# A hybrid attention/state-space trunk on one core: the scan's own-chunk product made with exchanged operands in three of four head groups

## The chip, the cores and the metric

The kernel runs on one core of one Trainium2 chip. The metric is the device time of one execution, in microseconds. All data is float32; large products are split into three float32r products (high by high, low by high, high by low part).

## The reference, cut to what matters

The program is two mixer layers (an attention layer, then a Mamba-2 scan layer), each with a gated feed-forward behind it, for one sequence of 512 tokens and a model width of 1024. The change touches only the scan of the second mixer:

```python
def step(state, inp):                       # one chunk of 128 tokens
    xc, dtc, bc, cc = inp
    cum = jnp.cumsum(dtc * A, axis=1)
    seg = cum[:, :, None] - cum[:, None]
    L = jnp.exp(jnp.where(tril, seg, -jnp.inf))
    xdt = xc.astype(f32) * dtc[..., None]
    cb = jnp.einsum('btgn,bsgn->btsg', cc, bc)
    y_diag = jnp.einsum('btsgh,bsghp->btghp', cb[..., None] * L, xdt)
    y_off = jnp.einsum('btgn,bghpn->btghp', cc, state) * jnp.exp(cum)[..., None]
    decay = jnp.exp(cum[:, -1:] - cum)
    new_state = (state * jnp.exp(cum[:, -1])[..., None, None]
                 + jnp.einsum('bsgn,bsghp->bghpn', bc, xdt * decay[..., None]))
    return new_state, y_diag + y_off
```

There are 32 heads of width 64 in four groups of eight, four chunks of 128 tokens, and a state of 128 per head. `y_diag` is the chunk's own y. After the scan, y gets a skip term, is multiplied by silu(z), normalised over its group, and projected.

## The kernel before

The instructions of each engine are written out by hand and ordered with semaphores; there is no scheduler. The scan part is unrolled: the outer loop runs over the head groups g = 0 to 3, the inner over the chunks k = 0 to 3. `last` means g = 3.

For each (g, k) the tensor engine (PE) does, in this order: `chunk_products(g, k + 1)` (two small products that give C·B and the turned B of the next chunk, lines 995 and 996); filler of place 0; a wait for `y_done` of the chunk before; the state's share of y (line 1062, bank 3) and the state's update (line 1065, bank 4); **the chunk's own y** (line 1071, bank 2): eight products, one for each head, with the 128x128 decay matrix `Lx` stationary and the 64 columns of scaled x, `xdt`, moving; filler of place 1; `to_features(g, k - 1)`, four transposes of the finished y of the chunk before (line 1003); filler of place 2. A float32 product of this kind is two instructions in the trace, so eight products are 16 there.

Filler is, in groups 0 to 2, the projection of z for the next group (line 1019): 24 products with 512 columns for each chunk, in thirds of eight. The table `places` puts the thirds at (none; two; one) for k = 0, (one; one; one) for k = 1 and 2, and (two; one; none) for k = 3. In group 3 the filler is the first half of the output projection (lines 476 to 478).

The vector engine (DVE) collects y in `ybuf`: state's share times decay (line 2067, not for k = 0), state update (2069, 2070, or 2072 for k = 0), plus the own y from bank 2 (2076), plus the skip term (2078, not for k = 0), times `zs` = silu(z) (2081), which signals `y_done`. The scalar engine (ACT) runs, for each (g, k): at k = 0 `split_hi` (1116, high part of a weight chunk); `z_copy` (1453); `decays(g, k + 1)` (1417, eight times, and 1423), which gives the decay matrices of the next chunk; `stage(g, k + 2)` (1408); at k = 0 of groups 1 to 3 the silu of z for the whole group (1482, with a table load); at k = 3 another `split_hi`; and then, waiting for `y_done`, the square of y (1503). GpSimd (POOL) scales x and multiplies `Lx` with C·B (2251 to 2259).

PSUM has eight banks. In the scan, banks 0 and 5 take z, 2 to 4 the parts of y, 6 and 7 the small products and the transposes. Bank 1 holds a tile of the first z projection, read by the four silu of line 1513 before the scan begins, and is next used in group 3.

Of the kernel before, what the change touches and what calls it, by code (L numbers as in the profile page):

```python
# [23 lines left out]
F32 = mybir.dt.float32  # L24
# [4 lines left out]
ACT = mybir.ActivationFunctionType  # L29
AX = mybir.AxisListType.X  # L30

P = 128
# [9 lines left out]
SH, SG, SHP, SP_, SN = 32, 4, 8, 64, 128  # L42
# [106 lines left out]
def trunk(nc, wstream, xT_in, cols_in, rows_in, pos_in, cw1_in, cw2_in, ident_in, tri_in, cmask_in, out):  # L149
    with ExitStack() as ctx:  # L150
# [3 lines left out]
        def sem(name):  # L154
            return ctx.enter_context(nc.semaphore(name))


        class Region:
# [29 lines left out]
        a = Region(scratch_at)  # L188
# [70 lines left out]
        zs = a.take("zs", [P, TT, GW])  # L259
        dt_at = a.end + 2 * TT * SH * 4  # L260
        dtb = a.take("dtb", [P, 10, TT * SH])
        dt_f = a.take("dt_f", [SH, SEQ])
        ex_at = a.end
        ex = a.take("ex", [P, 3, TT * SH])
# [62 lines left out]
        cum_copied, cumT_mm, cumT_done, rows_stored = map(  # L327
            sem, ("cum_copied", "cum_transposed", "cumT_copied", "cum_rows_stored"))
        row_landed = [sem("even_row_landed"), sem("odd_row_landed")]
        half_free, cs_read = sem("first_weights_free"), sem("cmp_scores_read")  # L330
        gate_in, gate_done, hh_done, hl_done = map(sem, ("gate_normed", "gate_done", "hidden_hi_done", "hidden_lo_done"))
        vec, pool_self = map(sem, ("vector_step", "pool_step"))
# [138 lines left out]
        def _(pe):  # L471
# [534 lines left out]
            def group(g, last):  # L1006
                def z_part(tt, third):

                    if third == 0:
                        if tt == 0:  # L1010
                            pe.wait_ge(lo_done, g * 2 + (n0 + 3))
                        pe.wait_ge(evac, g * 4 + (t0 + 4 + tt - 1))
                    t = slice(tt * P, (tt + 1) * P)
                    for m in range(8 * third, 8 * third + 8):
                        kt, pss = divmod(m, 3)
                        slot, w = (n0 + kt // 4) % 2, slice((kt % 4) * 512, (kt % 4 + 1) * 512)
                        if m == 12 and tt == 0:
                            pe.wait_ge(lo_done, g * 2 + (n0 + 4))
                        ins = mm(ps[:, z_bank_of(tt), :], (xh, xl, xh)[pss][:, kt, t], (wh, wh, wl)[pss][:, slot, w],  # L1019
                                 start=m == 0, stop=m == 23)  # L1020
                        if tt == 3 and m in (11, 23):
                            ins.then_inc(products, 2)
                        elif m == 23:
                            ins.then_inc(z_mm, 1)


                def half_product(t, ks):

                    c, m = divmod(t, 2)
                    n = CHUNK["ssm_out"] + c  # L1030
                    bank = half_bank(t)
                    if ks[0] == 0:
                        if t < 2:
                            pe.wait_ge(evac, EVAC["ssm_out"] - 1 + (t == 0))
                        pe.wait_ge(lo_done, n + 1)
                        after(pe, half_stored, t - 2)
                    for kt in ks:
                        if t == 0 and kt % 2 == 0:
                            pe.wait_ge(yl_done, kt // 2 + 1)
                        w = slice(kt * 256 + m * P, kt * 256 + (m + 1) * P)  # L1040
                        hi, lo = ys(kt)
                        ins = split_product(ps[:, bank, :].rearrange("p (a b) -> p a b", b=P), (wh[:, n % 2, w], wl[:, n % 2, w]),
                                            (hi, lo), kt == 0, kt == FIRST_KT - 1)
                    if ks[-1] == FIRST_KT - 1:
                        ins.then_inc(products, 1)

                places = {0: ((), (0, 1), (2,)), 1: ((0,), (1,), (2,)), 2: ((0,), (1,), (2,)), 3: ((0, 1), (2,), ())}
                for k in range(TT):
                    if k < 3 or not last:
                        chunk_products(g, k + 1)  # L1050

                    def z_at(place):
                        for third in () if last else places[k][place]:
                            z_part(k, third)
                        for t in FILL_AT.get((k, place), ()) if last else ():
                            half_product(*t)
                    z_at(0)
                    after(pe, y_done, g * 4 + k)
                    pe.wait_ge(xdt_done, g * 12 + 3 * (k + 1))
                    if k:  # L1060
                        pe.wait_ge(state_done, g * 3 + k)
                        mm(ps[:, 3, :], bc[:, k, 1, :], state[:, :], start=True, stop=True)  # L1062
                    if k < 3:
                        after(pe, state_done, g * 3 + k)
                        mm(ps[:, 4, :], btst[:, k % 2, :], xdd[:, k % 2, :], start=True, stop=True
                           ).then_inc(state_mm, 1)
                    for q in range(2):
                        pe.wait_ge(m_built, g * 8 + (2 * k + q + 1))
                        for h in range(4):
                            x = slice((4 * q + h) * SP_, (4 * q + h + 1) * SP_)  # L1070
                            ins = mm(ps[:, 2, x], Lx[:, k % 2, q, h, :], xdt[:, k % 2, x], start=True, stop=True)  # L1071
                        ins.then_inc(y_mm, 1)
                    z_at(1)
                    if k or not isinstance(g, int) or g:
                        to_features(g, k - 1)
                    z_at(2)
                if last:
                    half_product(6, range(FIRST_KT))
                    half_product(7, range(FIRST_KT))
                    to_features(g, 3)  # L1080
# [27 lines left out]
        def _(act):  # L1108
# [346 lines left out]
            def group(g, last):  # L1455
                first = isinstance(g, int) and g == 0
                for k in range(TT):
                    if k == 0 and not last:
                        split_hi(n0 + 3, g, 2)
                    if k:  # L1460
                        if not last:
                            z_copy(g, k - 1)
                    elif not first:
                        z_copy(g, -1)
                    if last and k == 0:
                        stage(g, 2)
                        act.wait_ge(products, 2 * CHUNK["ssm_out"])
                        act.wait_ge(yT_done, 2 * TT)
                        rows_hi(4)
                        rows_hi(6)  # L1470
                    if last and k >= 2:
                        half_copy(2 * k - 3)
                        split_hi(CHUNK["ssm_out"] + k)
                    if k < 3 or not last:
                        decays(g, k + 1)
                    if not last or k == 1:
                        stage(g, k + 2)
                    if k == 0:
                        if not first:
                            act.wait_ge(evac, g * 4 + (t0 + 4))  # L1480
                            act.wait_ge(y_done, g * 4)
                            A(zs[:, :, :], zraw[:, :, :], ACT.Silu).then_inc(z_silu, 1)
                    if k == 3 and not last:
                        split_hi(n0 + 4, g, 2)
                    if last and k:
                        half_copy(2 * k - 2)
                    if last and k == 0:
                        split_hi(CHUNK["ssm_out"] + 1)
                    if last and k == 1:
                        act.wait_ge(yT_done, 3 * TT)  # L1490
                        rows_hi(8)
                        rows_hi(10)
                    if last and k == 3:
                        last_rows_hi(0)
                        last_rows_hi(1)
                    if (g, k) == (SG - 3, 2):
                        act.wait_ge(yT_done, TT)
                        rows_hi(0)
                    if (g, k) == (SG - 2, 1):
                        rows_hi(2)  # L1500
                    act.wait_ge(y_done, g * 4 + (k + 1))
                    after(act, y_sq, g * 4 + k)
                    A(ysq[:, :], ybuf[:, k % 2, :], ACT.Square, accum_out=yst[:, k % 2, 0:1]).then_inc(y_sq, 1)
# [31 lines left out]
        def _(dve):  # L1535
# [508 lines left out]
            def group(g, last):  # L2044
# [4 lines left out]
                for k in range(TT):  # L2049
# [21 lines left out]
                    if k == 0:  # L2071
                        dve.tensor_copy(state[:, :], ps[:, 4, :]).then_inc(state_done, 1)
                    dve.wait_ge(y_mm, g * 8 + 2 * (k + 1))
                    dve.wait_ge(xdt_done, g * 12 + 3 * (k + 1))
                    V.wait(dve)
                    step(TTo(y, y if k else dxs[:, k % 2, :], ps[:, 2, :], ALU.add))
# [291 lines left out]
```

## Time and profile before

| what | us |
|---|---|
| median of three runs | 1465.36 |
| lowest and highest run | 1463.93, 1466.76 |
| profiled execution, span from first to last instruction | 1463.8 |
| of it, PE busy by the page | 1448.1 |
| scan groups 0 to 2, from 879 to 992 | 113 |
| scan group 3, from 992 to 1045 | 53 |

The page lists no separate device time for the profiled execution; its span is 1.6 below the median of the runs. The page is read from the top: busy shares, then the chain that ended last, then the groups of instructions. PE's ends are modelled in this profile, so waits on PE are read from the starts of its instructions, in the timeline.

### The profile page before, as it was taken

How to read it: one execution, taken by the hardware profiler on the slowest of the kernel's cores; microseconds unless marked ns; L12 is line 12 of the kernel's file. 1: busy time of each engine (PE TensorE's matmuls, PEld its weight loads, DVE VectorE, ACT ScalarE, POOL GpSimd, SP SyncE). 2: the span in 40 equal slices, each digit the busy share in tenths (PEclk: the TensorE clock that was granted, in tenths of full speed). 3: DMA queues.
4: the chain of work that ended last, by engine and by line, in shares of the span. 5: the costliest groups of instructions: out<-in, count | busy, mean ns of one | idle time of the engine just before them, and what ended most of it. 6: DMA issues, size and time to landing. Idle time of an engine off the chain costs nothing.

```text
span 1463.8 us, 19574 instructions
## 1 busy us (share of the span) xinstructions
PE 1448.1 (99%) x7362; PEld 1189.1 (81%) x7362; DVE 833.8 (57%) x1143; ACT 614.7 (42%) x998; POOL 253.5 (17%) x278
## 2 busy tenths in 40 slices
PE   9999999999999999999999999999999999999999
PEld 6878888788888888888888877777888888888887
DVE  5797787864644444333587756789544544444231
ACT  6467676644323222222233356778314322222121
POOL 4324423103000000000000018766103000000000
PEclk9999999999999999999999999999999999999999
DMA  9201010221322322332232233323132222232322
GB/s 340 87 30 45 14 59 30 87 74 72 101 101 86 109 92 90 111 103 98 86 115 86 86 131 116 115 101 115 59 115 86 87 99 101 86 111 90 115 86 86
DMA packets 23342, 139.19 MB, mean 95 GB/s; under 512 B 2672, under 2 KB 3440, under 8 KB 8944
## 3 DMA queue, kind: packets, MB, share of 16 engines
q1 hardware_dynamic: 20544, 127.54, 24.9%
q10 hardware_dynamic: 2736, 10.81, 2.1%
q8 instruction: 40, 0.66, 0.2%
q14 instruction: 22, 0.18, 0.0%
HBM read 136.18 MB, written 2.16 MB: 95 GB/s over the span
## 4 chain that ended last, share of the span: by engine, by line
PE 91%; DVE 3%; ACT 3%; POOL 1%; issue 1%; DMA 0%; SPq 0%; ACTq 0%; DVEq 0%; POOLq 0%
PE ps L476 24%; PE ps L477 24%; PE ps L478 24%; PE ps L835 4%; PE ps L1019 3%; PE ps L813 2%; PE ps L793 2%; PE ps L1071 1%; PE ps L702 1%; PE ps L737 1%; PE ps L738 1%; DVE sm L1790 1%; PE ps L1062 1%; PE ps L809 1%; ACT seg L1417 1%
## 5 line engine op out<-in xcount | busy, mean ns | idle before, releaser
L1547 DVE TENSOR_TENSOR wl<-wraw,wh 128x2048 fp32r<-128x2048 f32 x111 | 254.8, 2296 | 246.3 <-ACT wh L1116 246.3
L476 PE MATMUL ps<-xh,wh 128*128 128x512 f32 (+2 forms) x912 | 358.0, 392 | 0.0
L478 PE MATMUL ps<-xh,wl 128*128 128x512 f32 (+2 forms) x912 | 355.1, 389 | 0.0
L477 PE MATMUL ps<-xl,wh 128*128 128x512 f32 (+2 forms) x912 | 355.0, 389 | 0.0
L1116 ACT ACTIVATE wh<-wraw 128x2048 fp32r<-128x2048 f32 x111 | 211.7, 1907 | 178.3 <-PE ps L478 176.6
L477 PEld LDWEIGHTS ps<-xl,wh 128*128 128x128 f32 (+2 forms) x912 | 170.1, 187 | 36.9 <-issue 0.7
L476 PEld LDWEIGHTS ps<-xh,wh 128*128 128x128 f32 (+2 forms) x912 | 170.0, 186 | 36.9 <-issue 0.7
L478 PEld LDWEIGHTS ps<-xh,wl 128*128 128x128 f32 (+2 forms) x912 | 170.0, 186 | 36.9
L476 PE MATMUL ps<-hh,wh 128*128 128x512 f32 x352 | 136.9, 389 | 0.0
L477 PE MATMUL ps<-hl,wh 128*128 128x512 f32 x352 | 136.9, 389 | 0.0
L478 PE MATMUL ps<-hh,wl 128*128 128x512 f32 x352 | 136.9, 389 | 0.0
L2155 POOL TENSOR_TENSOR sqacc<-sqacc,sq 128x512 f32<-128x512 f32 x32 | 46.3, 1448 | 420.8 <-ACT sq L1125 418.2
L1186 ACT ACTIVATE hh<-hid 128x512 f32 (+1 forms) x44 | 27.8, 632 | 173.9 <-DVE hid L1634 173.9
L1181 ACT ACTIVATE gate<-gate 128x512 f32<-128x512 f32 x44 | 27.7, 632 | 138.9 <-DVE gate L1626 138.9
L476 PEld LDWEIGHTS ps<-hh,wh 128*128 128x128 f32 x352 | 66.1, 188 | 13.8
L478 PEld LDWEIGHTS ps<-hh,wl 128*128 128x128 f32 x352 | 66.1, 188 | 13.8
L477 PEld LDWEIGHTS ps<-hl,wh 128*128 128x128 f32 x352 | 66.1, 188 | 13.5
L1292 ACT ACTIVATE Pm<-ps,sm 128x128 f32<-128x128 f32 (+3 forms) x128 | 66.3, 526 | 20.1 <-DVE sm L1790 19.5
L1626 DVE TENSOR_TENSOR gate<-ps,tmp 128x512 f32<-128x512 f32 x44 | 29.9, 687 | 71.1 <-PE ps L478 71.0
L1300 ACT ACTIVATE PT<-ps 128x256 f32<-128x256 f32 (+3 forms) x64 | 45.1, 705 | 55.7 <-PE ps L793 55.2
L1790 DVE TENSOR_REDUCE sm<-ps 128x2 f32<-128x256 f32 (+3 forms) x64 | 52.7, 823 | 14.5 <-PE ps L740 12.2
L1951 DVE SCALAR_TENSOR_TENSOR tmp<-raw,cols,tmp 128x511 f32<-128x511 f32 (+2 forms) x72 | 54.0, 750 | 8.6 <-DVE tmp L1949 1.3
(301 smaller groups left out, 2364.3 us busy)
## 6 DMA issues: line engine op xcount, KB each, us to landing
wraw<-wstream SPq DMA_DIRECT2D x111, 1024.0 KB, 4.7
rowc<-cum_rows ACTq DMA_DIRECT2D x16, 512.0 KB, 3.6
cw<-cw_in SPq DMA_DIRECT2D x1, 4096.0 KB, 14.0
xT<-xT_in SPq DMA_DIRECT2D x8, 256.0 KB, 6.4
part<-xT_in ACTq DMA_DIRECT2D x1, 2048.0 KB, 8.9
out<-xT SPq DMA_DIRECT2D x8, 256.0 KB, 6.6
wraw<-wstream SPq DMA_DIRECT2D x2, 512.0 KB, 8.2
wraw<-wstream SPq DMA_DIRECT2D x3, 256.0 KB, 5.5
```

Of the source, the lines that this page charges most:

```text
L476: mm(o, wa[0], xa[0], start=start, stop=False)
L477: mm(o, wa[0], xa[1], start=False, stop=False)
L478: return mm(o, wa[1], xa[0], start=False, stop=stop)
L835: ins = mm(ps[:, 7, :], (xh, xl, xh)[pss][:, kt, t], (wh, wh, wl)[pss][:, slot, w], start=m == 0, stop=m == 23)
L1019: ins = mm(ps[:, z_bank_of(tt), :], (xh, xl, xh)[pss][:, kt, t], (wh, wh, wl)[pss][:, slot, w], start=m == 0, stop=m == 23)
L1116: A(wh[:, n % 2, :], wraw[:, n % 2, :], ACT.Copy).then_inc(hi_done, 1)
L1292: A(Pm[:, S % LAG, b, 0:w], src, ACT.Exp, bias=sm[:, 4, m + b:m + 1 + b], accum_out=sm[:, 4, m + 4 + b:m + 5 + b]).then_inc(expd, 1)
L1300: A(probsT(i)[:, h % 2], ps[:, 4:6, 0:(i + 1) * P].rearrange("p b (j q) -> p b j q", q=P), ACT.Copy).then_inc(pT_done, 1)
L1547: TTo(wl[:, s, :], wraw[:, s, :], wh[:, s, :].bitcast(F32), ALU.subtract).then_inc(lo_done, 1)
L1790: dve.tensor_reduce(sm[:, 4, m:m + 2], both, AX, ALU.max, negate=True).then_inc(negmax, 1)
L1951: ins = STT(out=c[:, d:], in0=x[:, 0:SEQ - d], scalar=w(3 - d), in1=c[:, d:], op0=ALU.mult, op1=ALU.add)
L2155: TTo(sqacc[:, :], sqacc[:, :], sq[:, mt % 2, :], ALU.add).then_inc(acc_done, 1)
```

## The change

In groups 0 to 2 the operands of the own y are exchanged: `xdt` (128x64) is stationary and `Lx` (128x128) moves. The result is the turned y of a head, 64 partitions by 128 tokens. Two heads share 128 partitions: head h goes to partitions 0 to 63 or 64 to 127, by `h % 2`, and four pairs of heads fill bank 1. ACT copies bank 1 into a new tile `ydT`, PE turns it back with four transposes into bank 2, and DVE reads bank 2 as before. The transposes stand behind the filler of place 1 and ahead of `to_features`; ACT's copy stands behind `stage(g, k + 2)`. At (0, 0) PE also waits until bank 1's tile of z has been read. Group 3 is as it was.

```diff
--- before.py
+++ after.py
@@ -259,6 +259,7 @@
         zs = a.take("zs", [P, TT, GW])
         dt_at = a.end + 2 * TT * SH * 4
         dtb = a.take("dtb", [P, 10, TT * SH])
+        ydT = nc.alloc_sbuf_tensor_at("ydT", [P, 4, P], F32, offset=a.end)
         dt_f = a.take("dt_f", [SH, SEQ])
         ex_at = a.end
         ex = a.take("ex", [P, 3, TT * SH])
@@ -327,6 +328,7 @@
         cum_copied, cumT_mm, cumT_done, rows_stored = map(
             sem, ("cum_copied", "cum_transposed", "cumT_copied", "cum_rows_stored"))
         row_landed = [sem("even_row_landed"), sem("odd_row_landed")]
+        ydT_copied, yd_mm = sem("own_chunk_y_copied"), sem("own_chunk_y_turned")
         half_free, cs_read = sem("first_weights_free"), sem("cmp_scores_read")
         gate_in, gate_done, hh_done, hl_done = map(sem, ("gate_normed", "gate_done", "hidden_hi_done", "hidden_lo_done"))
         vec, pool_self = map(sem, ("vector_step", "pool_step"))
@@ -1064,13 +1066,25 @@
                         after(pe, state_done, g * 3 + k)
                         mm(ps[:, 4, :], btst[:, k % 2, :], xdd[:, k % 2, :], start=True, stop=True
                            ).then_inc(state_mm, 1)
+                    if (g, k) == (0, 0):
+                        pe.wait_ge(evac, t0 + 2)
                     for q in range(2):
                         pe.wait_ge(m_built, g * 8 + (2 * k + q + 1))
                         for h in range(4):
                             x = slice((4 * q + h) * SP_, (4 * q + h + 1) * SP_)
-                            ins = mm(ps[:, 2, x], Lx[:, k % 2, q, h, :], xdt[:, k % 2, x], start=True, stop=True)
+                            if last:
+                                ins = mm(ps[:, 2, x], Lx[:, k % 2, q, h, :], xdt[:, k % 2, x], start=True, stop=True)
+                            else:
+                                pair = slice((2 * q + h // 2) * P, (2 * q + h // 2 + 1) * P)
+                                half = slice((h % 2) * SP_, (h % 2 + 1) * SP_)
+                                ins = mm(ps[half, 1, pair], xdt[:, k % 2, x], Lx[:, k % 2, q, h, :], start=True, stop=True)
                         ins.then_inc(y_mm, 1)
                     z_at(1)
+                    if not last:
+                        pe.wait_ge(ydT_copied, g * 4 + (k + 1))
+                        for pair in range(4):
+                            ins = pe.transpose(ps[:, 2, pair * P:(pair + 1) * P], ydT[:, pair, :], ident[:, :])
+                        ins.then_inc(yd_mm, 1)
                     if k or not isinstance(g, int) or g:
                         to_features(g, k - 1)
                     z_at(2)
@@ -1475,6 +1489,10 @@
                         decays(g, k + 1)
                     if not last or k == 1:
                         stage(g, k + 2)
+                    if not last:
+                        act.wait_ge(y_mm, g * 8 + 2 * (k + 1))
+                        after(act, yd_mm, g * 4 + k)
+                        A(ydT[:, :, :], ps[:, 1, :].rearrange("p (b n) -> p b n", b=4), ACT.Copy).then_inc(ydT_copied, 1)
                     if k == 0:
                         if not first:
                             act.wait_ge(evac, g * 4 + (t0 + 4))
@@ -2071,6 +2089,8 @@
                     if k == 0:
                         dve.tensor_copy(state[:, :], ps[:, 4, :]).then_inc(state_done, 1)
                     dve.wait_ge(y_mm, g * 8 + 2 * (k + 1))
+                    if not last:
+                        dve.wait_ge(yd_mm, g * 4 + (k + 1))
                     dve.wait_ge(xdt_done, g * 12 + 3 * (k + 1))
                     V.wait(dve)
                     step(TTo(y, y if k else dxs[:, k % 2, :], ps[:, 2, :], ALU.add))
```

PE at the border from group 0 to group 1, before. L1019 is filler, L1003 `to_features`, L995 and L996 `chunk_products`, L1065 the state's update, L1071 the own y (eight products in one row):

```order
L1019 MATMUL ps<-wl,xh 128x512
L1003 MATMUL ps<-ident,ybuf 128x128 x4
L995 MATMUL ps<-bc 128x128
L996 MATMUL ps<-ident,bc 128x128
L1065 MATMUL ps<-xdd,btst 128x512
L1071 MATMUL ps<-xdt,Lx 128x64 x8
L1019 MATMUL ps<-wh,xh 128x512
```

The same place in the changed kernel; its lines there are 1021, 1086 (new), 1005, 997, 998, 1067, 1080 and 1021:

```order
L1021 MATMUL ps<-wl,xh 128x512
L1086 MATMUL ps<-ident,ydT 128x128 x4
L1005 MATMUL ps<-ident,ybuf 128x128 x4
L997 MATMUL ps<-bc 128x128
L998 MATMUL ps<-ident,bc 128x128
L1067 MATMUL ps<-xdd,btst 128x512
L1080 MATMUL ps<-Lx,xdt 64x128 x8
L1021 MATMUL ps<-wh,xh 128x512
```

Four transposes of `ydT` stand behind the last filler of chunk 3, and the own y has its operands exchanged; nothing else on PE moved.

ACT at k = 0 of group 1, before, from the split ahead of `z_copy` to the square of y:

```order
L1116 ACTIVATE wh<-wraw 128x2048
L1453 ACTIVATE zraw<-ps,stat 128x512
L1417 ACTIVATE seg<-rowc,cum 128x128 x8
L1423 ACTIVATE Lx<-seg 128x512 x2
L1430 DMA rowc<-cum_rows 128x1024
L1408 ACTIVATE bc<-BCf 128x256
L1482 ACT_TABLE_LOAD
L1482 ACTIVATE zs<-zraw 128x2048
L1503 ACTIVATE ysq,yst<-ybuf 128x512
```

And in the changed kernel:

```order
L1130 ACTIVATE wh<-wraw 128x2048
L1467 ACTIVATE zraw<-ps,stat 128x512
L1431 ACTIVATE seg<-rowc,cum 128x128 x8
L1437 ACTIVATE Lx<-seg 128x512 x2
L1444 DMA rowc<-cum_rows 128x1024
L1422 ACTIVATE bc<-BCf 128x256
L1495 ACTIVATE ydT<-ps 128x512
L1500 ACT_TABLE_LOAD
L1500 ACTIVATE zs<-zraw 128x2048
L1521 ACTIVATE ysq,yst<-ybuf 128x512
```

The copy stands between the staging of chunk k + 2 and the silu of z.

## Rows read from the trace of the kernel before

**Rows 1.** The page's part 1: busy us, share of the span, instructions.

```profile
PE 1448.1 (99%) x7362; PEld 1189.1 (81%) x7362; DVE 833.8 (57%) x1143; ACT 614.7 (42%) x998; POOL 253.5 (17%) x278
```

**Rows 2.** Timeline of PE: start, duration, instruction, idle before; groups 0 to 1.

```profile
911.61 1.89 PE L1071 MATMUL ps<-xdt,Lx 128*128 128x64 f32 x16
913.31 0.48 PE L1019 MATMUL ps<-wh,xl 128*128 128x512 f32 x1
...
915.24 0.60 PE L1003 MATMUL ps<-ident,ybuf 128*128 128x128 f32 x4
915.67 0.39 PE L995 MATMUL ps<-bc 128*128 128x128 f32 x2
...
916.00 1.02 PE L1065 MATMUL ps<-xdd,btst 128*128 128x512 f32 x2
...
918.57 0.48 PE L1019 MATMUL ps<-wh,xh 128*128 128x512 f32 x1
```

**Rows 3.** Timeline of PE, column halves in the attention part.

```profile
300.54 0.44 PE L809 MATMUL ps<-pcT,vz 128*64 128x128 f32 x4
...
301.78 0.44 PE L737 MATMUL ps<-kB,qA 128*128 128x384 f32 x1
...
302.90 0.44 PE L809 MATMUL ps<-pcT,vz 128*64 128x128 f32 x4
...
304.58 0.44 PE L737 MATMUL ps<-kB,qA 128*128 128x384 f32 x1
```

**Rows 4.** Timeline, group 0, k = 0: PE's first filler, ACT's last step ahead.

```profile
881.55 0.48 PE L1019 MATMUL ps<-wh,xh 128*128 128x512 f32 x1
```

```profile
886.05 0.40 ACT L1408 ACTIVATE bc<-BCf 128x256 f32<-128x256 f32 x1
```

**Rows 5.** The instructions of line 1453, ACT's copies of a PSUM bank: ns min/median/max.

```profile
L1453 ACT ACTIVATE zraw<-ps,stat x12: 667/670/689, 887.3 to 993.6; 128x512 f32<-128x512 f32 x12
```

**Rows 6.** Timeline of DVE: y of (0, 3), then of (1, 0).

```profile
914.99 0.69 DVE L2081 TENSOR_TENSOR ybuf<-ybuf,zs 128x512 f32<-128x512 f32 x1
...
925.84 1.45 DVE L2081 TENSOR_TENSOR ybuf<-ybuf,zs 128x512 f32<-128x512 f32 x1 [2.32 <-ACT zs L1482]
```

**Rows 7.** Timeline of PE: entry to group 3, (2, 3) to (3, 0).

```profile
993.01 1.13 PE L1065 MATMUL ps<-xdd,btst 128*128 128x512 f32 x2 [0.55 <-DVE ybuf L2081]
```

**Rows 8.** Timeline of ACT, group 1: k = 0, then k = 1 to its `stage`.

```profile
915.71 0.63 ACT L1503 ACTIVATE ysq<-ybuf 128x512 f32<-128x512 f32 x1 [2.58 <-DVE ybuf L2081]
...
922.10 0.40 ACT L1408 ACTIVATE bc<-BCf 128x256 f32<-128x256 f32 x1
...
927.32 0.63 ACT L1503 ACTIVATE ysq<-ybuf 128x512 f32<-128x512 f32 x1 [1.58 <-DVE ybuf L2081]
...
933.32 0.40 ACT L1408 ACTIVATE bc<-BCf 128x256 f32<-128x256 f32 x1
```

**Rows 9.** Timeline of PE, group 1, from k = 0 to k = 1.

```profile
922.38 0.66 PE L1003 MATMUL ps<-ident,ybuf 128*128 128x128 f32 x4
...
926.65 0.39 PE L1019 MATMUL ps<-wh,xl 128*128 128x512 f32 x1
927.34 1.13 PE L1062 MATMUL ps<-state,bc 128*128 128x512 f32 x2 [0.30 <-DVE ybuf L2081]
...
930.86 0.48 PE L1019 MATMUL ps<-wl,xh 128*128 128x512 f32 x1
```

**Rows 10.** PE around its longest wait in the scan, and the shorter one at 89.

```profile
1022.73 0.66 PE L1003 MATMUL ps<-ident,ybuf 128*128 128x128 f32 x4 [1.79 <-DVE ybuf L2020]
...
1024.32 0.63 PE L477 MATMUL ps<-yl,wh 128*128 128x512 f32 x1
1024.74 0.63 PE L478 MATMUL ps<-yh,wl 128*128 128x512 f32 x1
```

```profile
89.30 0.44 PE L737 MATMUL ps<-kB,qA 128*128 128x384 f32 x1 [1.11 <-ACT Pm L1292]
```

**Rows 11.** One stretch: us, each engine's busy time, PE's granted clock, DMA share, GB/s.

```profile
1024.00:1027.00 3.00, 3.00 (x9) 2.32 (x8) 2.90 (x5) 0.00 (x0) 3.00 (x3) 0.50 0.27 107
```

## What the change does to the time: the prediction

> **What bounds the kernel now.** I read the busy shares first: PE counts as busy 99% of the span and no other engine over 57% [rows 1]. That sends the reader to PE, with a warning: its ends are modelled, so a wait of half a microsecond hardly shows there. The timeline by starts is what to read. In the scan PE runs one fixed list, own y, filler, transposes, filler, and each dependent step on DVE and ACT has filler on PE as its cover. The cover is tight. Only three waits stand in groups 0 to 2: PE stands 0.30 at (1, 1) and 0.55 at the entry to group 3 by the profile's own count [rows 7, 9], and (2, 1) is like (1, 1). The question is whether PE's list becomes shorter, and whether a longer dependent chain still fits under the filler.
>
> **PE's own work.** Before, eight products take 1.70 from their start to the next instruction's (911.61 to 913.31) [rows 2]. The exchanged form, a 64-column stationary, 128 columns moving, alternately on the two halves, already runs in the attention part, lines 809 and 813. There 20 such instructions take 1.24 (300.54 to 301.78) and 28 take 1.68 (302.90 to 304.58) [rows 3]. So one costs 0.055, and a block 0.14 besides. Sixteen make 0.88 + 0.14 = 1.02; I take 1.05, since nothing loads the first half ahead. That saves 0.65 in eleven chunks. In (0, 0) I put 0.3, as POOL hands over the second half of `Lx` late there: 7.45 in all. Bounds: 0.8 saved if the switch is free (1.70 less 0.88), and a loss of 0.2 if the halves don't run side by side (sixteen at 0.11, and the 0.14).
> Four transposes cost 0.43 (915.24 to 915.67) [rows 2], twelve times 5.15. PE's list is thus shorter by 2.3, a fifth of a microsecond in each chunk. DVE reads the same bank at the same price; its time doesn't change, only its start.
>
> **What the Trainium skill says of this.** In "TensorEngine Tiling (Array Packing)", "When to Use Tiling" names just this exchange for a moving side of 64 columns and promises a factor of two; by it a block would fall to 0.85 and the sum below by up to 2.4. The rows give 1.02, so I keep 1.05. The same page, "PSUM Bottleneck", says that the copy out of PSUM may become the bound after such a gain. The waits below are that case.
>
> **ACT's copy.** Twelve copies of 128x512 from PSUM; the nearest rows are 0.67 each [rows 5]. They overlap their neighbours by about 0.1 on ACT, so I take 0.6. ACT has time for them in total. But the copy waits behind `stage(g, k + 2)`, and PE then waits for the copy at the end of place 1. That gives three kinds of wait.
>
> **(a) ydT at (0, 0).** ACT's `stage` ends at 886.05 + 0.40 = 886.45, so the copy ends at 887.05 [rows 4]. PE begins the filler at 881.55 less 0.3, and sixteen products of filler take 3.8 (eight take 1.93, 913.31 to 915.24 [rows 2]): 885.05. PE waits 2.0.
>
> **(b) y_done at the three group borders.** This is the change's main fault. `places` gives no filler at place 2 of k = 3 nor at place 0 of k = 0. Before, the own y of (g, 3) was done at 913.31 and DVE's `y_done` came at 914.99 + 0.69 = 915.68 [rows 6], 2.37 later, beneath the eight fillers of place 1; PE needed it at 916.00 and didn't wait [rows 2]. Now bank 2 is full only after those fillers and the transposes. Between it and the need stand `to_features` (0.43) and `chunk_products` (915.67 to 916.00, 0.33). PE waits 2.37 + 0.05 - 0.76 = 1.65, at three borders 4.95, less the 0.55 that it waits at the last one now [rows 7]: 4.4.
>
> **(c) ydT at k = 0 of groups 1 and 2.** Count from `y_done` of (g, 3). ACT takes the square, then split, z copy, decays, stage, until 922.10 + 0.40 = 922.50, 6.8 after 915.68 [rows 6, 8]; with the copy 7.4. PE: state update and own y take 2.57 (916.00 to 918.57) [rows 2], less 0.65, and the filler 3.8, in all 5.8. PE waits 1.65, twice 3.3. The wait absorbs the late low part of the weights that DVE makes at this place.
> What is late next is (g, 1)'s need of `y_done` of (g, 0). Before, PE stood from 926.65 + 0.23 to 927.34, 0.46, behind the silu and DVE's last step, which ends at 925.84 + 1.45 = 927.29 [rows 6, 9], 11.6 after the border. Now it ends 0.6 later, at 12.2, behind the copy. PE arrives at 7.45 + 0.43 + 4.5 (922.38 to 926.88 [rows 9]) = 12.4. So that wait goes: -0.9 for both groups.
>
> **(d) ydT at k = 1 of groups 1 and 2.** ACT again starts at `y_done` (927.32) and ends `stage` at 933.72, with the table of exp loaded back in between [rows 8]: 6.4, with the copy 7.0, so 19.2 on the clock of (c). PE: 12.4, then 3.52 (927.34 to 930.86 [rows 9]) less 0.65, then eight fillers, 1.93: 17.2. PE waits 2.0, twice 4.0. At k = 2 and 3, and at (0, 1), no table is loaded; ACT's copy is ready 1 or more before PE asks.
>
> Sum without the clock: -2.3 + 2.0 + 4.4 + 3.3 - 0.9 + 4.0 = **10.5**. The extra wait at (0, 0) for bank 1 costs nothing: the four silu of line 1513 are through before POOL hands over `Lx`. In group 3 every chain starts at `y_done` of (2, 3) and moves as a whole, so nothing is given back.
>
> **The clock.** After a wait of 1.79 the same product's starts are 0.42 apart (1024.32 to 1024.74) instead of 0.24 [rows 2, 10], and the granted clock of that stretch is 0.50, so 1.2 GHz instead of 2.4 [rows 11]. Some eight products ran so: 1.6 lost. After a wait of 1.11 line 737 took its 0.44 as elsewhere [rows 3, 10]. The changed kernel has eight waits of 1.6 to 2.1, on both sides of that case. A fall after the borders of groups 0 and 1, or after a wait (c), would be hidden under the next wait for ydT; at (0, 0), at both (d) and after the last border it costs its whole 1.6. I take two of these four, 3.2; bounds 0 and 6.4. The total is 13.7.
> The Trainium skill ("TensorE: Matmul & The Clock Gate", "Why this matters for your kernels") warns only of idle gaps longer than any here; by it the sum stays 10.5 and the time would be 1475.9. The row of the 1.79 wait speaks against it, so I don't follow it.
>
> **How the numbers follow.** The profiled span is 1463.8, 1.6 below the median and 0.1 below the lowest run, so the sum is added to the median: 1465.4 + 13.7 = **1479.1**. Below 0.2% (2.9) a measurement of this kernel can't tell from no change.
>
> **Rivals.** *The halves don't run side by side* (the change doesn't do what it says): 0.85 more than my 1.05 in each chunk, felt in the seven chunks where PE isn't waiting for ACT anyway, 6.0: 1485. The pace of lines 809 and 813 speaks against it. 0.08.
> *The waits are shorter*: DVE and ACT overlap more than by my ends, half of (a) to (d) shows, and no fall of the clock: 1465.4 - 3.2 + 6.9 = 1469 to 1474. 0.17.
> *All waits hide* (the other side): if ACT finds its copy done by the end of place 1, and `y_done` at the borders comes in time, only PE's list counts, -2.3 and the 0.9: 1462.2. It decides as soon as (a) to (d) together stay under 3.2; they come to 13.7, and (b) is a plain count of steps with no filler behind them. 0.06.
> *The Trainium skill's rule on the clock*, as above, is 1475.9, inside the forecast. 0.25 of the forecast's share.
> The forecast's own range, 1474.5 to 1482, gets 0.63, and gains and losses that cancel 0.06.
> Over 80%: **1470.5 to 1486**. Faster 0.06, same 0.06, slower 0.88.
>
> **What would show it.** The own y in about 1.05 between starts; PE waits named after ACT ydT at k = 0 of groups 0 to 2 and k = 1 of groups 1 and 2, of 1.6 to 2.1 each, none at k = 2 and 3; waits for DVE ybuf of some 1.6 at each border; the period from border to border 38.2 before and near 42 after; a granted clock of 0.5 in up to four short stretches, and group 3 as long as before. I am wrong if the copy stands ready at k = 0 and 1, if DVE begins y at (g, 3) before the transposes, or if a block takes 1.7.

## The result, and the profile after

| kernel | median us | lowest, highest | ratio, 95% interval |
|---|---|---|---|
| before, same chip | 1465.48 | 1463.93, 1466.76 | |
| after | 1475.28 | 1472.71, 1477.65 | 1.0068 [1.0058, 1.0079] |

The changed kernel is slower by 9.8; by the interval, by 8.5 to 11.6. The forecast was 1479.1 within 1470.5 to 1486, with 0.88 on slower. The median agrees with the sum without the clock, 10.5. The 3.2 put on top of it for the clock does not show in the median.

The profiled execution took 1472.71, its span is 1470.9, so 7.1 more than the span before. The page's busy shares, in the columns of [rows 1]:

```profile
PE 1444.6 (98%) x7410; PEld 1179.7 (80%) x7410; DVE 829.8 (56%) x1143; ACT 620.6 (42%) x1010; POOL 249.8 (17%) x278
```

PE has 48 instructions more, the twelve times four transposes, and is busy 3.5 less. ACT has the twelve copies more. The list of waits shows what the shorter work was paid with. PE in the scan, after the change: total us, number of times, longest.

```profile
PE ps L1086 <- ACT ydT L1495: 5.7, 5, 1.8
PE ps L1067 <- DVE ybuf L2101: 4.6, 3, 1.5
PE ps L1005 <- DVE ybuf L2038: 1.8, 1, 1.8
PE ps L1080 <- POOL Lx L2279: 0.5, 1, 0.5
PE ps L1021 <- DVE wl L1565: 0.4, 2, 0.2
```

Before, this list held only 1.8, 0.6 and 0.5 for DVE's `ybuf` (line 1003, [rows 10]; line 1062, [rows 9]; line 1065, [rows 7]). The first two rows are what the change costs. They are the five waits for the copy and the three at the borders, where only the last border had 0.5 before. The 0.5 for `Lx` stands inside the own y of (0, 0). The list before has no such row, but the block took longer there too, 2.15 (879.40 to 881.55) against 1.70 elsewhere. The 0.4 for `wl`, the weights' low part, is new as well.

Timeline of PE after, at (0, 0), at the border from group 0 to 1, and at (1, 0); columns as in [rows 2]:

```profile
885.76 0.66 PE L1086 MATMUL ps<-ident,ydT 128*128 128x128 f32 x4 [1.81 <-ACT ydT L1495]
```

```profile
915.36 0.60 PE L1086 MATMUL ps<-ident,ydT 128*128 128x128 f32 x4
915.79 0.60 PE L1005 MATMUL ps<-ident,ybuf 128*128 128x128 f32 x4
916.23 0.39 PE L997 MATMUL ps<-bc 128*128 128x128 f32 x2
916.45 0.27 PE L998 MATMUL ps<-ident,bc 128*128 128x128 f32 x1
918.25 1.12 PE L1067 MATMUL ps<-xdd,btst 128*128 128x512 f32 x2 [1.53 <-DVE ybuf L2101]
```

```profile
923.71 0.50 PE L1021 MATMUL ps<-wh,xh 128*128 128x512 f32 x1 [0.20 <-DVE wl L1565]
...
925.55 0.66 PE L1086 MATMUL ps<-ident,ydT 128*128 128x128 f32 x4 [0.65 <-ACT ydT L1495]
```

Then (1, 1), with the state's update, the own y and the first filler behind it:

```profile
931.36 1.02 PE L1067 MATMUL ps<-xdd,btst 128*128 128x512 f32 x2
932.31 1.09 PE L1080 MATMUL ps<-Lx,xdt 128*64 128x128 f32 x16
933.34 0.50 PE L1021 MATMUL ps<-wl,xh 128*128 128x512 f32 x1
933.67 0.39 PE L1021 MATMUL ps<-wh,xh 128*128 128x512 f32 x1
...
936.77 0.66 PE L1086 MATMUL ps<-ident,ydT 128*128 128x128 f32 x4 [1.32 <-ACT ydT L1495]
```

DVE at the same border, to set beside [rows 6]:

```profile
916.05 0.69 DVE L2096 TENSOR_TENSOR ybuf<-ybuf,ps 128x512 f32<-128x512 f32 x1 [2.21 <-PE ps L1086]
916.78 0.69 DVE L2098 TENSOR_TENSOR ybuf<-ybuf,dxs 128x512 f32<-128x512 f32 x1
917.50 0.69 DVE L2101 TENSOR_TENSOR ybuf<-ybuf,zs 128x512 f32<-128x512 f32 x1
```

DVE stands 2.21 for the transposes of 915.36. Its three steps end at 918.19, and PE's next dependent product starts at 918.25. Nothing lies between: the border is one chain from the transposes through DVE to PE.

**Ledger.** A period is the time from the start of one own y to the start of the next, read from PE's timeline. It doesn't depend on modelled ends. "Forecast" is made of the prediction's own terms.

| period | before | after | difference | forecast |
|---|---|---|---|---|
| (0, 0) to (0, 1) | 11.60 | 13.81 | +2.21 | +2.13 |
| (0, 1) to (0, 3), two | 20.61 | 20.30 | -0.31 | -0.44 |
| borders 0 to 1, 1 to 2, each | 5.26 | 6.92 | +1.66 | +1.43 |
| border 2 to 3 | 6.07 | 6.83 | +0.76 | +0.88 |
| k = 0 to 1, groups 1, 2, each | 12.29 | 13.01 | +0.72 | +0.97 |
| k = 1 to 2, groups 1, 2, each | 9.82 | 11.23 | +1.41 | +1.78 |
| k = 2 to 3, groups 1, 2, each | 10.78 | 10.63 | -0.15 | -0.22 |
| sum, groups 0 to 2 | 114.6 | 124.5 | +9.95 | +10.5 |
| group 3, (3, 2) to (3, 3) | 17.58 | 15.94 | -1.64 | |

The last row is a stretch of low clock that the profiled execution before had [rows 11] and this one had not. The scan also began 1.13 earlier (878.27 for 879.40), where the change does nothing; in the twelve experiments it began at 879.75 to 881.40, so this is scatter between executions. So 9.95 - 1.64 - 1.13 = 7.2 is the difference of the two spans, and 9.8 that of the medians.

### The profile page after: what moved, and what is told of

Same layout as the page of the kernel before. It is cut to its first block, busy times and chain, and to the rows that moved or that the text cites. A ratio compares the mean times of both kernels' runs of the same rounds, so it can differ in the third digit from the quotient of the medians.

```text
span 1470.9 us, 19706 instructions
## 1 busy us (share of the span) xinstructions
PE 1444.6 (98%) x7410; PEld 1179.7 (80%) x7410; DVE 829.8 (56%) x1143; ACT 620.6 (42%) x1010; POOL 249.8 (17%) x278
## 4 chain that ended last, share of the span: by engine, by line
PE 89%; ACT 4%; DVE 3%; issue 2%; POOL 1%; DMA 1%; SPq 0%; ACTq 0%; DVEq 0%; POOLq 0%
PE ps L478 23%; PE ps L480 23%; PE ps L479 23%; PE ps L837 4%; PE ps L1021 3%; PE ps L815 2%; PE ps L795 2%; ACT seg L1431 1%; PE ps L704 1%; DVE sm L1808 1%; PE ps L739 1%; PE ps L740 1%; DVE Pm L1819 1%; PE ps L811 1%; PE ps L1080 0%
## 5 line engine op out<-in xcount | busy, mean ns | idle before, releaser
L1808 DVE TENSOR_REDUCE sm<-ps 128x2 f32<-128x256 f32 (+3 forms) x64 | 52.7, 823 | 14.5 <-PE ps L742 12.2
```

The lines of the kernel that those rows point to most:

```text
L1808: dve.tensor_reduce(sm[:, 4, m:m + 2], both, AX, ALU.max, negate=True).then_inc(negmax, 1)
```

## The experiments

The theory: the price is the two chains, own y to ACT's copy to the transposes, and the transposes to DVE to the border, each without enough filler. The rivals: the exchanged product or the transposes themselves cost it; or the clock does. "Scan" below is the time from the first own y to DVE's `y_done` of (2, 3): 113.6 before, 123.5 after. Line numbers are those of each kernel, a few off from after's.

**Run 1. The exchanged product without the turning.** Its y isn't turned back, so that part of the work is left out.

```diff
-    ins = mm(ps[half, 1, pair], xdt[:, k % 2, x], Lx[:, k % 2, q, h, :], ...)
+    ins = mm(ps[half, 2, pair], xdt[:, k % 2, x], Lx[:, k % 2, q, h, :], ...)
-    (the wait, the four transposes and yd_mm; ACT's copy; DVE's wait for yd_mm)
```

> The exchanged product alone: the turned y goes straight to bank 2 and DVE adds it as it stands; the copy to ydT and the turning back are left out. Theory (the loss is waits on a longer dependent chain, the product itself is a gain): twelve blocks 0.56 shorter each, read in the changed kernel, 6.7, of which the waits for y_done at (1, 1) and (2, 1) take back about 1: 1459.5 to 1461. Rival (the switch to column halves costs more than the rows show, and is the loss): not under 1465, up to 1470.

Measured 1463.54 against 1465.54, ratio 0.9986 [0.9976, 0.9996]: faster, but by 2.0 and not by the 4.4 or more expected. The list did become shorter: periods without a wait went from 9.82 to 9.25 and from 10.79 to 10.24, so 0.56 for each block. The chains on DVE did not. The borders 0 to 1 and 1 to 2 kept their length (5.23 and 5.33 for 5.26). (0, 0) took 12.14 for 11.60, as PE waited 0.54 for the weights' low part; runs 5 and 9 have the same wait, and run 3, whose edit at (0, 0) is that of run 5, has not, so it looks like scatter. From k = 0 to 1 the period did not shrink (12.29, now 12.45), since `y_done` of (1, 0) comes when the silu is through, whatever PE does. At the border to group 3 PE waited 1.94 instead of 0.55. DVE and POOL there, in this kernel:

```profile
987.43 0.69 DVE L2085 TENSOR_TENSOR ybuf<-ybuf,ps 128x512 f32<-128x512 f32 x1
988.15 1.80 DVE L2087 TENSOR_TENSOR ybuf<-ybuf,dxs 128x512 f32<-128x512 f32 x1
989.98 1.63 DVE L2090 TENSOR_TENSOR ybuf<-ybuf,zs 128x512 f32<-128x512 f32 x1
```

```profile
988.11 2.96 POOL L2268 TENSOR_TENSOR Lx<-Lx,cbm 128x512 f32<-128x512 f32 x2
```

The two steps with both inputs in SBUF take 1.80 and 1.63 instead of 0.69, just while POOL multiplies `Lx`. The step before them, with one input in PSUM, takes its 0.69, but it ends as POOL's multiply begins. As PE came earlier, so did DVE's steps, and they met POOL's.

**Run 2. The turning without the exchanged product.** Here the old operands' product goes to bank 1, and is then copied and turned; the y that comes out is therefore another one.

```diff
-    ins = mm(ps[half, 1, pair], xdt[:, k % 2, x], Lx[:, k % 2, q, h, :], ...)
+    ins = mm(ps[:, 1, x], Lx[:, k % 2, q, h, :], xdt[:, k % 2, x], ...)
```

> The product as before, but into bank 1, then copied and turned as in the changed kernel (its y is turned once too often, so the values differ). Theory: all waits stay, PE's list is 0.56 longer in the chunks where PE does not wait for ydT anyway (seven): 1475.3 + 4 = 1479. Rival (the exchanged product is the loss): 1466 to 1470, no more than the twelve turnings of 0.43.

Measured 1478.88, ratio 1.0091 [1.0072, 1.0109], as expected. The border waits are the same 4.6 in total, those for the copy 4.3, and the scan takes 127.5. With run 1 this parts the change: the exchange gives 2.0 without the turning and 3.6 with it, the copy and the turning cost 11.7 with the exchange and 13.3 without it.

**Run 3. The copy earlier.** In `decays(g, k + 1)` it goes between the eight steps of line 1431 and the two exp.

```diff
-    (the wait, after(...) and A(ydT, ps[:, 1, :], Copy) behind stage(g, k + 2))
     in decays(g, j, turned), after seg_built:
+    if turned:
+        turned()
```

> The changed kernel with the ACT copy ahead of the two exp of decays instead of behind stage. Theory: the waits of PE for ydT at (0, 0), 1.8, at (1, 0) and (2, 0), 0.65 each, at (1, 1) and (2, 1), 1.3 each, go, but the waits for the weights' low part and for y_done at k = 1 keep some tenths: 1475.3 - 5.3 = 1470. The three border waits of 1.53 stay. Rival (the copy is late because ACT is full, wherever it stands): 1474 to 1476, the wait moves to Lx or y_done.

Measured 1471.6, ratio 1.0045 [1.003, 1.006], 1.6 more than expected. All five waits for the copy are gone; those at the borders grew from 4.6 to 5.9. The scan is 4.7 shorter than after's, not the 5.7 of the waits. The profiled execution also has a stretch of low clock in group 3 (17.54 for 15.94), which after's has not. The cause of the longer borders is again on DVE, line 2100 (2098 in after), beside POOL's multiply:

```profile
915.86 0.69 DVE L2098 TENSOR_TENSOR ybuf<-ybuf,ps 128x512 f32<-128x512 f32 x1 [2.21 <-PE ps L1086]
916.58 1.09 DVE L2100 TENSOR_TENSOR ybuf<-ybuf,dxs 128x512 f32<-128x512 f32 x1
```

```profile
914.59 2.54 POOL L2281 TENSOR_TENSOR Lx<-Lx,cbm 128x512 f32<-128x512 f32 x2 [2.05 <-ACT Lx L1439]
```

The first of the two DVE steps, with its input in PSUM, lies wholly beside POOL's and takes 0.69 all the same. The second takes 1.09.

**Run 4. Filler at the borders.** Only the table of places is changed: a third of the filler moves to place 2 of k = 3.

```diff
-  3: ((0, 1), (2,), ())}
+  3: ((0,), (1,), (2,))}
```

> The changed kernel with the filler of k = 3 placed (one; one; one) instead of (two; one; none), so that eight products stand between the turning and the next group. Theory: the border waits of 1.53 go, three times, 4.6: 1470.7, if the weights' low part is not late by then. Rival (another dependence holds PE at the border, the weights of the next z): 1474 to 1476, with PE waiting for wl at k = 0.

Measured 1472.59, ratio 1.0047 [1.0029, 1.0065], 1.9 more than expected. In the scan the step came as expected: the waits at the borders fall from 4.6 to 0.4, the 5.7 for the copy stay, and the scan is 4.8 shorter. But group 3 has a stretch of low clock in this execution (17.52 for 15.94), which takes 1.6 back.

**Run 5. Both together.**

> The changed kernel with the copy ahead of the exp and the filler of k = 3 placed (one; one; one). Theory: with all waits on the longer chain gone only the list of PE counts: twelve times 0.43 - 0.56, less the waits of 0.46, 0.3 and 0.55 of the kernel before where they go too: 1475.3 - 5.3 - 4.6 = 1465.4, between 1463 and 1467, no clear gain over the kernel before. Rival (the waits are independent of place): above 1470.

Measured 1467.94 against 1465.4, ratio 1.0021 [1.0011, 1.003]: 2.5 more than expected. I had added the two gains, and they don't add: the scan takes 116.2, 7.3 less than after's, where the two alone gave 9.5. Of the missing 2.2, some 0.8 stands at (0, 0), the wait for the weights' low part named in run 1. The rest stands at the borders to groups 2 and 3. DVE and POOL ahead of the border to group 3:

```profile
991.78 0.69 DVE L2098 TENSOR_TENSOR ybuf<-ybuf,ps 128x512 f32<-128x512 f32 x1 [0.64 <-PE ps L1086]
992.50 1.76 DVE L2100 TENSOR_TENSOR ybuf<-ybuf,dxs 128x512 f32<-128x512 f32 x1
994.30 1.64 DVE L2103 TENSOR_TENSOR ybuf<-ybuf,zs 128x512 f32<-128x512 f32 x1
```

```profile
992.41 2.97 POOL L2281 TENSOR_TENSOR Lx<-Lx,cbm 128x512 f32<-128x512 f32 x2
```

PE then waits 1.67 for line 2103. The instructions of that skip term in all twelve chunks (ns min/median/max), first in this kernel, then in after:

```profile
L2100 DVE TENSOR_TENSOR ybuf<-ybuf,dxs x12: 691/1347/1761, 896.8 to 1040.6; 128x512 f32<-128x512 f32 x12
```

```profile
L2098 DVE TENSOR_TENSOR ybuf<-ybuf,dxs x12: 691/693/1361, 896.5 to 1046.4; 128x512 f32<-128x512 f32 x12
```

After's waits had mostly kept these steps out of POOL's way. Where the waits go, more of the steps meet it.

**Run 6. The same filler in the kernel before**, the control:

> The kernel before with the filler of k = 3 placed (one; one; one): control for the place of the filler by itself. Theory: the one border wait of 0.55 goes, nothing else: 1465. Rival (the filler's place is worth something by itself, whatever the y chain): over 3 less or more.

Measured 1464.56, ratio 0.9998 [0.9988, 1.0007]. The moved third is worth little without the change. By the traces groups 0 to 2 are 1.6 shorter (112.95 for 114.57) and (3, 0) to (3, 1) is 0.6 longer. So most of the 2.7 that the third gives in run 4 is the border's bare chain.

**Runs 7 and 8. The copy doubled**, once at k = 0 and 1, once at k = 2 and 3. In either, PE's transposes wait for the second copy.

```diff
+  if k in (0, 1):          # in the other kernel (2, 3)
+      A(ysq[:, :], ps[:, 1, :], ACT.Copy).then_inc(ydT_copied, 1)
```

> The changed kernel with the ACT copy of bank 1 made twice at k = 0 and 1 of groups 0 to 2 (six more copies of 0.5 to 0.6), the second one into a scratch tile; ydT counts as copied behind it. Theory: those chains bound PE, so each copy shows: (0, 0) 0.5, (1, 0) and (2, 0) 0.5, (1, 1) and (2, 1) 0.5 and what the later silu adds: 1475.3 + 2.5 to 3.5 = 1478 to 1479. Rival (ACT's copy is hidden): 1475.3.

> The same at k = 2 and 3: also six more copies. Theory: there the copy is ready 1.2 before PE asks, so nothing shows: 1475.3, within 1. Rival (ACT's total work counts, not the place): as much as with the copies at k = 0 and 1, 2.5 to 3.5 more.

Measured 1478.09, ratio 1.0092 [1.0076, 1.0107], and 1475.99, ratio 1.0073 [1.0058, 1.0089]. The same work on ACT costs 2.8 by the medians at k = 0 and 1, and nothing in the scan at k = 2 and 3 (123.52 for 123.50). So it isn't ACT's load, but how late the copy is at two places. This is the clearest test of the steps (a), (c) and (d), and in kind they hold. In size run 7 met its forecast partly by luck. In its trace the periods grew by 0.5 at k = 0 of groups 1 and 2, as forecast, but by only 0.2 at k = 1 of those groups, where 0.5 and more was forecast. At (0, 0) the period grew by 2.14: 0.55 is the longer wait, and some 1.6 is a stretch of low clock behind it that the forecast did not have. So the copies themselves cost about 1.9.

**Run 9. The skip term first.** DVE adds `dxs`, which is ready early, before it waits for the own y; the chain behind the transposes is one step shorter.

```diff
+    if k:
+        step(TTo(y, y, dxs[:, k % 2, :], ALU.add))
     dve.wait_ge(y_mm, ...); dve.wait_ge(yd_mm, ...)
     step(TTo(y, y if k else dxs[:, k % 2, :], ps[:, 2, :], ALU.add))
-    if k:
-        step(TTo(y, y, dxs[:, k % 2, :], ALU.add))
```

> The changed kernel, and DVE adds the skip term ahead of the own y instead of behind it, so that two steps instead of three stand behind the turning at k = 1 to 3. Theory (the border wait is a count of DVE steps behind the turning): 0.72 less at each of three borders, 2.2: 1473.1; the waits for ydT stay. Rival (DVE's chain isn't what the border waits for, or the step is stretched where it stands now): 1475.3.

Measured 1472.17, ratio 1.0043 [1.0027, 1.0058], a gain of 3.1 on after: the borders shrink from 6.92 to 6.23, one DVE step of 0.69, as expected, and the wait in group 3 from 1.8 to 0.7, which the forecast of 1473.1 did not count.

**Runs 10 to 12. All three edits, and the kernel before with two and with one of them.**

> The kernel with early copy and border filler, and the skip term first. Read in that kernel: the borders still stand 0.2, 0.6 and 1.8 over the control with the filler alone, and k = 0 to k = 1 0.85 over it in groups 0 to 2, as DVE's two last steps run beside POOL's Lx and take 1.6 to 1.8 instead of 0.69. Theory (DVE beside POOL holds the rest): a step of 0.7 to 1.7 goes from each border chain: 1467.9 - 3 = 1465, between 1463.5 and 1466. Rival (the exchanged product and its turning hold the rest on PE): 1467.9.

> The kernel before with the filler of k = 3 placed (one; one; one) and the skip term first: does the kernel before gain from the same two mends? Theory: there nothing waits for y_done any more but (2, 1) by some tenths, so 0 to 0.5 less than with the filler alone: 1464.3. Rival (the mends are worth the same everywhere): 1461 to 1462.

> The kernel before with the skip term first and its filler where it was: which of the two mends brings the 3.5 that both together brought to the kernel before. Theory (y_done is late for PE at two places only): 0.55 at the last border, 1.05 at PE's wait for the scaled y in group 3, and with that wait down to 0.7 no fall of the clock behind it, 1.6 in the executions that have one: 1465.7 - 1.6 to 3.2 = 1462.5 to 1464. Rival (the filler's place brings it): 1465.5.

| kernel | own y | median | n | ratio, 95% interval |
|---|---|---|---|---|
| early copy, border filler, skip first | exchanged | 1462.01 | 9 | 0.9974 [0.9964, 0.9984] |
| border filler, skip first | as before | 1461.99 | 8 | 0.9974 [0.9963, 0.9984] |
| skip first | as before | 1463.54 | 10 | 0.9992 [0.9982, 1.0001] |

The kernel before, run beside the first two, had a median of 1465.85, and beside the third 1464.64.

All waits of PE in the scan, first with the exchanged product, then without it:

```profile
PE ps L1005 <- DVE ybuf L2040: 0.7, 1, 0.7
PE ps L1080 <- POOL Lx L2281: 0.5, 1, 0.5
```

```profile
PE ps L1003 <- DVE ybuf L2020: 0.8, 1, 0.8
```

Of after's 13.0 of waits 1.2 are left. Both kernels beat the kernel before, by 3.8 and 3.9, and tie with each other. So the exchanged product, with its copy and its transposes fully covered, gives nothing here that can be told from the noise, about 1.5 either way. Chunk by chunk it is 0.15 shorter (9.68 for 9.82, 8.81 for 8.97), but 0.4 to 0.5 longer at k = 0 to 1 of groups 1 and 2 (12.19 and 12.11 for 11.78 and 11.61) and 0.17 longer at (0, 0). From the first own y to that of (3, 0) the two come to 112.6 and 112.7. That leaves the filler and the skip term as the whole gain.

All three forecasts were off in size. Run 10 came 3 under its 1465. By the traces groups 0 to 2 are 4.6 shorter than in run 5, 0.85 of it the wait at (0, 0) that run 5 had by chance, and the wait in group 3, where the filler is the output projection, is 1.1 shorter. I had counted the shorter chain at the borders only. Run 11 came at 1461.99, not at 1464.3 but at the number of its rival. The rival's reason doesn't hold, though: the skip term first gave 5.9 on top of run 5 and 2.6 on top of run 6. The traces show where my count failed. Against run 6, groups 0 to 2 are only 0.2 shorter, as I had thought, but group 3 is 1.6 shorter. Run 12 is 1.1 under the kernel before measured beside it, where 1.6 to 3.2 was expected, and its interval includes no change. In its trace groups 0 to 2 are no shorter (114.7 for 114.6), and the period (3, 2) to (3, 3) is 14.94 for 17.58, with no stretch of low clock.

## Why the prediction was right, point by point

- **The block.** Forecast 1.05; measured 1.03 (932.31 to 933.34). But the way into the form costs too: the state's update ahead of it takes 0.95 from start to start (931.36 to 932.31), where it took 0.86 before (928.30 to 929.16). The first filler behind it takes 0.33, hardly more than the 0.31 of before. The net saving is 0.56, not 0.65. Run 1 gives the same 0.56. It is a small miss, 0.09 in each chunk where PE doesn't wait anyway. The rival of 1485, where the halves don't run side by side, is refuted, and the 0.85 of a full factor of two did not come either.
- **The transposes.** 0.43 forecast and measured (915.36 to 915.79).
- **(a), 2.0 at (0, 0).** Recorded 1.81; the period grew 2.21, forecast 2.13.
- **(b), 1.65 at each border.** Recorded 1.53, and by starts 1.69 (916.23 to 918.25 is 2.02, where 0.33 stood before). The chain is the one that was counted. Run 4 confirms its cause, since filler at that place takes the wait away. The border's period is 0.23 longer than forecast all the same: behind a wait the state's update takes 1.05 to the own y (918.25 to 919.30), and I had the 0.87 of before.
- **(c), 1.65 at k = 0 of groups 1 and 2.** The chain is right to 0.1: the transposes start 7.36 behind the border's `y_done` (918.19 to 925.55), forecast 7.4. The recorded waits are smaller, 0.65 for the copy and 0.20 for the weights, because the own y starts 0.19 later than counted and the filler runs longer with the weights' wait in it. The period is 0.25 short of the forecast, most of it the 0.23 that the border's has too much.
- **(d), 2.0 at k = 1.** Recorded 1.32, the period 0.37 short of the forecast. DVE's multiply ahead of it took 0.97, not the 1.45 of [rows 6], so `y_done` of (1, 0) came 11.6 behind the border's instead of 12.2. The 1.45 was itself a step stretched beside POOL's multiply, and I had carried it over as a fixed cost. POOL's row before, then after:

```profile
924.19 2.55 POOL L2259 TENSOR_TENSOR Lx<-Lx,cbm 128x512 f32<-128x512 f32 x2
```

```profile
926.70 2.54 POOL L2279 TENSOR_TENSOR Lx<-Lx,cbm 128x512 f32<-128x512 f32 x2
```

  Before, the multiply ran from 925.84 and lay beside POOL for 0.9; after, from 928.83, for 0.4.
- **The removed waits, -0.9.** They are gone.
- **Group 3 gives nothing back.** (3, 0) to (3, 2) takes 25.06 after and 25.08 before.
- **The clock, +3.2.** This is the term that was mis-sized. The profiled execution shows no stretch of low clock in the scan, behind eight waits. They were also shorter than the 1.6 to 2.1 forecast: 1.81 at (0, 0), 1.53 at the borders, 1.32 at (d) and 0.65 at (c). Two of the other four executions had a mean clock of 0.997 and took 1477.4 and 1477.7, so a few microseconds may be lost to it there; behind which waits is not shown, as neither was profiled. By the medians the term is about -0.2 (9.8 less 9.95), with the noise of the medians, over 1, in it. Before's profiled execution pays for one such stretch too [rows 11].

So the mechanism held, the waits on the two longer chains. That the sum without the clock came so near is partly luck: the borders took 0.23 more each than forecast, k = 0 and k = 1 0.25 and 0.37 less. The range held because its lower part was kept for the case without a fall.

## What to carry to other kernels

Where an engine has a fixed list with filler for cover, price an edit by the place where its result is needed, not by what it saves: 0.56 saved in each chunk was worth nothing next to a copy and transposes in the chain, and a copy doubled cost some 2 at k = 0 and 1, without the low clock behind it, and nothing at k = 2 and 3. Before putting a faster form of a product in, look at whether the chain behind it can be made shorter: moving an add that doesn't need the product ahead of the wait, and a third of the filler to the bare border, gave 3.9 together without touching the product; either alone gave no gain clear of the noise. When a wait is taken away, look at which engines then work at the same time that had not before.

## What the runs showed of the hardware

**DVE beside POOL.** A 128x512 float32 step of DVE with both inputs in SBUF took 0.69 alone, and 1.6 to 1.8 while POOL's two-input multiply ran (988.15 in run 1, 992.50 in run 5). A step with one input in PSUM kept its 0.69 though it lay wholly beside POOL's multiply (915.86 in run 3). The steps of this size that write `ybuf` in the scans of all fourteen traces agree. With both inputs in SBUF, some 170 that no POOL instruction overlapped took 0.69 each, and some 220 that one overlapped took 0.69 to 1.81, ten of them still 0.69. With an input in PSUM, all 390 took 0.67 to 0.69, the 327 beside a POOL instruction too. No experiment took POOL's work away, so this rests on the traces alone. The order in which a chain's steps stand thus sets its price: with the skip term first, the stretched add lies before the wait.

**The clock behind short waits.** The same wait of 1.8 in group 3 stood in nine of the traces, and its period, (3, 2) to (3, 3), came in two sizes: 17.5 to 17.6 in the kernel before and in runs 1, 3 and 4, 15.9 in after and in runs 2, 5, 6 and 7. So a fall costs 1.6 there, and the same wait had one in four of nine cases. With the wait at 0.7 to 0.8, in the last four runs, none had. Falls came behind others too, in runs 7 and 8. A stretch of run 7 and one of run 8, columns as in [rows 11]:

```profile
888.00:892.00 4.00, 4.00 (x16) 3.31 (x16) 1.53 (x3) 1.06 (x3) 1.61 (x3) 0.60 0.51 214
```

```profile
1008.00:1012.00 4.00, 4.00 (x12) 3.25 (x12) 3.73 (x4) 3.98 (x12) 4.00 (x4) 0.50 0.75 275
```

Before either, PE had waited:

```profile
887.88 0.66 PE L1086 MATMUL ps<-ident,ydT 128*128 128x128 f32 x4 [2.36 <-ACT ysq L1500]
```

```profile
1004.98 1.13 PE L1067 MATMUL ps<-xdd,btst 128*128 128x512 f32 x2 [1.52 <-DVE ybuf L2108]
```

Behind the second PE ran at 1.2 GHz instead of 2.4 until 1013, and the period was 15.74 instead of 12.58, 3.2 lost. Of this 2.0 came back: the wait of 1.8 in group 3 was gone, and its period was 13.96 for 15.94. In after the same wait, at 1001.82, had no fall behind it. The Trainium skill ("TensorE: Matmul & The Clock Gate", "Why this matters for your kernels") warns only of idle gaps longer than any of these. These rows show falls behind gaps of 1.5 to 2.4, in some executions and not in others; what decides between them, these runs don't tell.
